# Two channel convolutions of a hybrid decoder block, done later in the gate turns

## The chip, the core and the metric

One core of one Trainium2 chip runs the whole block as one program. The metric is device time in microseconds (us), the median of several executions. Engine names are those of the profile: PE (TensorE matmuls), PEld (TensorE weight loads, which overlap PE), DVE (VectorE), ACT (ScalarE), POOL (GpSimd), SP (the engine that issues the weight loads).

## The reference, cut to what matters

For 256 tokens and 2048 channels, one block computes a Mamba-2 mixer and an S5 mixer in parallel, merges them by sigmoid gates, and runs a gated MLP. The change touches only the path of the Mamba-2 mixer's B and C inputs:

```python
z, xbc, dt_raw, u, g_a, g_b = jnp.split(hn @ w_in[i], splits, axis=-1)
xbc = jax.nn.silu(causal_dwconv(xbc, conv_w, conv_b))      # 4 taps per channel
xs, bm, cm = jnp.split(xbc, [D_INNER_A, D_INNER_A + gn], axis=-1)
cb = jnp.einsum("bclgn,bcsgn->bgcls", Cc, Bc)               # per group of 8
y_diag = jnp.einsum("bgcls,bgrcls,bcsgrp->bclgrp", cb, decay_in, X)
```

`bm` and `cm` have 8 groups of 128 channels each. Group g's product `cb` is needed for the first time when group g's part of the mixer runs.

## The kernel before, in words

**Weights.** All weights stream through a ring of four slots in units of 128 x 1024 fp32. SP loads a unit into `raw` once DVE has finished with the slot's last unit. ACT rounds it to `whi` (`split_hi`, line 666), DVE makes `wlo = raw - whi` (`split_lo`, line 1107), and PE multiplies with both (lines 1822 to 1824 in the gate phase, 1783 and 1785 before it). ACT and DVE work up to four units ahead of PE. Each engine runs its instructions strictly in the order in which the program lists them, and all waits are on semaphores.

**Order of the phases.** The projection `u`, then 24 groups `zx`, then 8 groups `bc` (each a B tile and a C tile, turns of four groups), then `gate` (8 turns of 8 units), `proj`, `glu`, `out`, `up`, `down`. During `zx` and `bc` the S5 scans run between the units on DVE. During `gate`, turn i also does the Mamba-2 mixer of group i.

**A `bc` group.** After PE has its sums, ACT copies one half out of PSUM (`hsum`, line 673) and DVE adds the halves (line 1112) into `cpad`, a tile with three zero columns ahead of the tokens. ACT computes the last tap with the bias (`group_tap`, line 776), from `cpad` into `bc`. DVE adds the other three taps for both tiles (`group_conv`, line 1303, six instructions). ACT applies Silu in place (`group_silu`, line 797). These pieces are listed one group behind: what belongs to group r stands in the turn of group r+1. Group 6's pieces stand in the last `bc` turn, group 7's in gate turn 0.

**A gate turn i.** In what follows "unit i.j" is unit j of gate turn i on PE. `hi(j)` and `lo(j)` in the code of turn i prepare the unit four later: `hi(0)` to `hi(3)` prepare i.4 to i.7, and `hi(4)` to `hi(7)` prepare (i+1).0 to (i+1).3. POOL loads the decay rows of three heads into each of two tiles (`dec`, line 442) as soon as PE has finished with them in the turn before. DVE scans them (`scan`, line 1416), ACT takes their exponential (line 853), DVE multiplies them with the masked `cb` (`blocks`, line 1422), PE forms the outputs (`heads`, lines 1908 and 1909), DVE adds the skip and multiplies by z (lines 1478 and 1481), ACT squares (line 895), DVE sums the squares (lines 1124 and 1486), and PE reduces them in the next turn behind its units 0 and 1 (`group_squares`, line 1829). ACT stages group i+1's B tile and x for PE (`stage`, lines 856 and 857), and PE makes `cb` and the transposes of x (lines 1924 to 1933) behind them. In gate turn 0, PE also finishes the last S5 block (`s5_products(7)`, line 1873) between its units 2 and 3; DVE's `s5_out` (line 1313) and ACT's first `stage` wait for it, and so does POOL with its second `dec` load.

The edit touches `group_tap`, `group_silu`, `stage` and `gate_turn` on ACT, `group_sums`, `group_conv`, `cpad_free` and `gate_turn` on DVE, and the operand of `cb` on PE.

Of the kernel before, what the change touches and what calls it, by code (L numbers as in the profile page):

```python
# [26 lines left out]
ds = bass.ds  # L27
# [81 lines left out]
def build_program(nc, a, out):  # L109
    ctx = ExitStack()  # L110
    with ctx:
# [77 lines left out]
        cpad = at("cpad", [P, 2, L + 4], F32, C + 4096)  # L189
        parm = at("parm", [P, N_PARM], F32, C + 6208)  # L190
# [465 lines left out]
        def _(act):  # L656
# [107 lines left out]
            def group_tap(name, i, r):  # L764

                _, per, quads, u0, g0 = phase(name)
                if name == "u" or name == "zx" and r % 2 == 0:
                    return
                act.wait_ge(sum_ready, i * per + (g0 + r + 1))
# [10 lines left out]
            def group_silu(name, i, r):  # L780
# [8 lines left out]
                elif name == "zx":  # L789
                    act.wait_ge(conv_done, i * 2 + (r // 2 + 1))  # L790
                    act.nop(nofuse=True)
                    to = zx[:, ds(i * 4 + (r - 1), 2), 1, :]
                    fn(to, to, ACTF.Silu).then_inc(xbc_done, 1)
                else:
                    act.wait_ge(conv_done, i * per + (12 + r + 1))
                    to = bc[:, ds(i * 4 + r, 1), :, :].rearrange("p o c n -> p (o c) n")
                    fn(to, to, ACTF.Silu).then_inc(xbc_done, 1)

# [45 lines left out]
            def gate_turn(i, prev, last=False):  # L844
# [10 lines left out]
                def stage(g):  # L855
                    fn(bst[:, :], bc[:, ds(g, 1), 0, :].rearrange("p o n -> p (o n)"), ACTF.Copy).then_inc(staged, 1)
                    fn(xst[:, :, :], zx[:, ds(g * TPG, TPG), 1, :], ACTF.Copy).then_inc(staged, 1)

                if prev is None:
# [10 lines left out]
                    group_silu("bc", 1, 3)  # L870
                    act.wait_ge(xbc_done, 20)
                    act.wait_ge(z_done, 12)
# [13 lines left out]
                hi(4)  # L886
                hi(5)
# [4 lines left out]
                hi(6)  # L892
                act.wait_ge(yz_ready, i + 1)
# [205 lines left out]
        def _(dve):  # L1099
# [215 lines left out]
            def group_sums(name, i, r):  # L1315
# [3 lines left out]
                elif name == "zx" and r % 2 == 0:  # L1319
                    add_halves(zx[:, ds(i * 4 + r, 2), 0, :], g0 + r, i * per)  # L1320
                else:
                    add_halves(cpad[:, :, 3:3 + L], g0 + r, i * per)

            def group_conv(name, i, r):
# [4 lines left out]
                if name == "u" or name == "zx" and r % 2 == 0:  # L1329
                    return  # L1330
                if name == "zx":
                    dve.wait_ge(tap_ready, i * 2 + (r // 2 + 1))
                else:
                    dve.wait_ge(tap_ready, i * per + (12 + r + 1))
# [6 lines left out]

            def cpad_free(name, i, r):

                if name == "bc":
                    dve.wait_ge(conv_done, i * 4 + (12 + r + 1))
# [60 lines left out]
            def gate_turn(i, prev, first_scan=False, next_scan=True):  # L1406
# [33 lines left out]
                if prev is None:  # L1440
# [4 lines left out]
                    group_conv("bc", 1, 3)  # L1445
# [23 lines left out]
                lo(4)  # L1469
                lo(5)  # L1470
                if prev is None:
                    dve.wait_ge(xbc_done, 20)
                    dve.wait_ge(z_done, 12)

# [278 lines left out]
        def _(pe):  # L1753
# [146 lines left out]
            def gate_turn(i, prev):  # L1900
# [22 lines left out]
                c = bc[:, ds(i, 1), 1, :].rearrange("p o n -> p (o n)")  # L1923
# [186 lines left out]
```

## Time and profile before

| | |
|---|---|
| median of 3 runs | 1679.96 us (1679.75 to 1681.75) |
| the profiled execution | 1680.3 us, of it 1678.6 us span |
| granted TensorE clock | 0.998 |
| PE busy | 1667.1 us, 99% |
| DVE busy | 1320.3 us, 79% |
| ACT busy | 962.7 us, 57% |
| gate turns 0 to 7 | from 431.7 to 641.7 us |

The profile is of one execution. A row of a timeline has the start, the time until the last of its instructions ended, the engine, the line, the operation and the tiles, and in square brackets how long the engine sat idle before it and what released it. Two instructions in a row on one engine can overlap a little, so the next start is often 0.1 us ahead of the last end.

### The profile page before, as it was taken

The page shows a single profiled execution, that of the slowest core. Times are in us where ns is not written, and L with a number is a line of the kernel's source. Part 1 is how long each engine was busy: PE and PEld are TensorE (multiplying, and loading weights), DVE is VectorE, ACT ScalarE, POOL GpSimd, SP SyncE. Part 2 cuts the span into 40 slices and gives each one's busy share as a digit, 9 for nine tenths or more (in the row PEclk, how much of TensorE's full clock was granted, in tenths as well). Part 3 has the DMA queues.
Part 4 walks back from the last instruction along what each step waited for, and adds up shares of the span by engine and source line. Part 5 has one row for each costly group of instructions (what it writes and reads, how often), then busy time and mean ns, then how long its engine had stood idle before and what let it go on. Part 6 is the DMA issues. An engine that isn't in the chain of part 4 may idle for free.

```text
span 1678.6 us, 24422 instructions
## 1 busy us (share of the span) xinstructions
PE 1667.1 (99%) x8340; PEld 1395.1 (83%) x8340; DVE 1320.3 (79%) x1685; ACT 962.7 (57%) x1271; POOL 216.4 (13%) x310
## 2 busy tenths in 40 slices
PE   9999999999999999999999999999999999999997
PEld 8888888888788888888888888888888888888886
DVE  7999999999998986545775868888878888845555
ACT  7676676766666667444557755444444444454553
POOL 7843342221000000000000200000000000000001
PEclk9999999999999999999999999999999999999999
DMA  7666766666666566656786577777777777666653
GB/s 254 213 197 199 204 206 200 193 188 190 194 217 231 191 219 189 199 191 201 239 254 232 174 233 241 243 241 244 242 244 241 245 232 248 225 194 195 191 189 123
DMA packets 174569, 358.49 MB, mean 214 GB/s; under 512 B 16880, under 2 KB 39584, under 8 KB 174368
## 3 DMA queue, kind: packets, MB, share of 16 engines
q1 hardware_dynamic: 162528, 338.26, 62.5%
q0 software_dynamic: 11248, 18.37, 4.6%
q8 instruction: 41, 0.67, 0.2%
q10 hardware_dynamic: 720, 0.93, 0.2%
q14 instruction: 32, 0.26, 0.0%
HBM read 335.41 MB, written 15.80 MB: 209 GB/s over the span
## 4 chain that ended last, share of the span: by engine, by line
PE 73%; DVE 2%; issue 0%; ACT 0%; DVEq 0%
PE psum L1822 22%; PE psum L1823 22%; PE psum L1824 22%; PE psum L1783 3%; PE psum L1785 2%; PE psum L1908 1%; DVE wlo L1107 0%; PE psum L1909 0%; DVE vn L1749 0%; PE psum L1933 0%; DVE bc L1303 0%; PE psum L1829 0%; PE psum L1924 0%; DVE dec L1416 0%; PE psum L1982 0%; PE psum L1979 0%
## 5 line engine op out<-in xcount | busy, mean ns | idle before, releaser
L1107 DVE TENSOR_TENSOR wlo<-raw,whi 128x1024 fp32r<-128x1024 f32 x580 | 709.6, 1230 | 321.3 <-ACT whi L666 314.0
L666 ACT ACTIVATE whi<-raw 128x1024 fp32r<-128x1024 f32 x580 | 611.9, 1058 | 577.1 <-PE psum L1824 455.1
L1783 PE MATMUL psum<-act,whi 128*128 128x512 f32 x1088 | 342.5, 396 | 0.0
L1822 PE MATMUL psum<-whi,nw 128*128 128x512 f32 x704 | 274.1, 389 | 0.0
L1824 PE MATMUL psum<-whi,nw 128*128 128x512 f32 x704 | 273.9, 389 | 0.0
L1823 PE MATMUL psum<-wlo,nw 128*128 128x512 f32 x704 | 273.9, 389 | 0.0
L1785 PEld LDWEIGHTS psum<-act,wlo 128*128 128x128 f32 x1088 | 204.4, 188 | 48.3
L1785 PE MATMUL psum<-act,wlo 128*128 128x256 f32 x1088 | 213.7, 278 | 0.0
L1783 PEld LDWEIGHTS psum<-act,whi 128*128 128x128 f32 x1088 | 165.6, 189 | 3.3 <-issue 2.8
L1824 PEld LDWEIGHTS psum<-whi,nw 128*128 128x128 f32 x704 | 132.1, 188 | 27.6
L1822 PEld LDWEIGHTS psum<-whi,nw 128*128 128x128 f32 x704 | 132.1, 188 | 27.3
L1823 PEld LDWEIGHTS psum<-wlo,nw 128*128 128x128 f32 x704 | 132.1, 188 | 27.3
L1822 PE MATMUL psum<-whi,act 128*128 128x512 f32 x352 | 138.8, 394 | 0.8 <-DVE wlo L1107 0.8
L1824 PE MATMUL psum<-whi,act 128*128 128x512 f32 x352 | 137.1, 390 | 0.0
L1823 PE MATMUL psum<-wlo,act 128*128 128x512 f32 x352 | 137.1, 389 | 0.0
L1822 PE MATMUL psum<-whi,ff 128*128 128x512 f32 x264 | 102.7, 389 | 0.0
L1823 PE MATMUL psum<-wlo,ff 128*128 128x512 f32 x264 | 102.7, 389 | 0.0
L1824 PE MATMUL psum<-whi,ff 128*128 128x512 f32 x264 | 102.7, 389 | 0.0
L1822 PEld LDWEIGHTS psum<-whi,act 128*128 128x128 f32 x352 | 66.1, 188 | 16.2 <-DVE wlo L1107 1.6
L1824 PEld LDWEIGHTS psum<-whi,act 128*128 128x128 f32 x352 | 66.1, 188 | 13.9
L1823 PEld LDWEIGHTS psum<-wlo,act 128*128 128x128 f32 x352 | 66.1, 188 | 13.1
L1303 DVE SCALAR_TENSOR_TENSOR fsum<-cpad,parm,fsum 128x256 f32<-128x256 f32 x176 | 76.9, 478 | 0.0
(251 smaller groups left out, 2300.3 us busy)
## 6 DMA issues: line engine op xcount, KB each, us to landing
raw<-in_w_up SPq DMA_DIRECT2D x176, 512.0 KB, 4.9
raw<-in_w_zx SPq DMA_DIRECT2D x96, 512.0 KB, 3.7
raw<-in_w_down SPq DMA_DIRECT2D x88, 512.0 KB, 3.8
raw<-in_w_gate SPq DMA_DIRECT2D x64, 512.0 KB, 5.6
raw<-in_w_proj SPq DMA_DIRECT2D x48, 512.0 KB, 4.4
raw<-in_w_bc SPq DMA_DIRECT2D x32, 512.0 KB, 3.7
raw<-in_w_glu SPq DMA_DIRECT2D x32, 512.0 KB, 4.4
raw<-in_w_out SPq DMA_DIRECT2D x32, 512.0 KB, 4.8
```

The lines of the kernel that those rows point to most:

```text
L666: fn(whi[:, s, :], raw[:, s, :], ACTF.Copy).then_inc(hi_ready, 1)
L1107: V.tensor_tensor(wlo[:, s, :], raw[:, s, :], whi[:, s, :], ALU.subtract).then_inc(lo_ready, 1)
L1303: ins = V.scalar_tensor_tensor(to[t], src, col(w, q * taps + k), to[t], ALU.mult, ALU.add)
L1783: mm(psum[:, b + t, :], whi[:, s, cols(t)], x, start=first, stop=False)
L1785: ins = mm(psum[:, b + t, L:2 * L], wlo[:, s, cols(t)], x[:, 0:L], start=False, stop=last)
L1822: mm(banks[:, t, :], x_hi, high[:, k], start=j == 0 and k == 0, stop=False)
L1823: mm(banks[:, t, :], x_hi, low[:, k], start=False, stop=False)
L1824: ins = mm(banks[:, t, :], x_lo, high[:, k], start=False, stop=last and k == 1)
L1908: mm(y, xtok[:, 0, x], dec[half][:, k, 0:L], start=True, stop=False)
```

## The change

Group 6 is no longer convolved in the last `bc` turn. Its sums go straight into the `bc` tile; in gate turn 1 ACT writes the last tap from there into `cpad` (`late_tap`, behind `hi(4)`), DVE adds the other taps out of place into `cpad` (`late_conv`, behind `lo(5)`), and ACT applies Silu to `cpad` (`late_silu`, behind `hi(6)`). Where group 6's B and C are used, in turns 5 and 6, they are read from `cpad`. Group 7's convolution moves on DVE from ahead of `lo(1)` to between `lo(4)` and `lo(5)` of gate turn 0, and its Silu on ACT from ahead of the first decay exponential to between `hi(4)` and `hi(5)`. The counts of the semaphores follow.

```diff
+        late_bc = {6: cpad}
+        late_count = {7: 7, 6: 8}
+        def bc_of(g, t):
+            return late_bc[g][:, t, 0:L] if g in late_bc else bc[:, g, t, :]
+        def bc_count(g):
+            return 12 + late_count.get(g, g + 1)
+        def comes_late(name, i, r):
+            return name == "bc" and i == 1 and r == 2
...
+            def late_tap(g):
+                act.wait_ge(sum_ready, phase("bc")[4] + g + 1)
+                for t in range(2):
+                    ins = fn(bc_of(g, t), bc[:, g, t, :], ACTF.Identity,
+                             scale=col("conv_a_w", (24 + 2 * g + t) * 4 + 3), bias=col("conv_a_b", 24 + 2 * g + t))
+                ins.then_inc(tap_ready, 1)
+            def late_silu(g):
+                act.wait_ge(conv_done, bc_count(g))
+                to = late_bc[g][:, :, 0:L]
+                fn(to, to, ACTF.Silu).then_inc(xbc_done, 1)
...
                     hi(1)
                     hi(2)
-                    group_silu("bc", 1, 3)
-                    act.wait_ge(xbc_done, 20)
-                    act.wait_ge(z_done, 12)
                     decay(0)
...
                 hi(4)
+                if i == 1:
+                    late_tap(6)
+                if prev is None:
+                    group_silu("bc", 1, 3)
+                    act.wait_ge(xbc_done, 19)
+                    act.wait_ge(z_done, 12)
                 hi(5)
...
                 hi(6)
+                if i == 1:
+                    late_silu(6)
                 act.wait_ge(yz_ready, i + 1)
...
+            def late_conv(g):
+                dve.wait_ge(tap_ready, bc_count(g))
+                for k in (2, 1, 0):
+                    for t in range(2):
+                        if k < 2:
+                            step.hold(but=1)
+                        to = bc_of(g, t)[:, 3 - k:L]
+                        ins = V.scalar_tensor_tensor(to, bc[:, g, t, 0:L - 3 + k],
+                                                     col("conv_a_w", (24 + 2 * g + t) * 4 + k), to, ALU.mult, ALU.add)
+                        if k or not t:
+                            step.begun(ins)
+                ins.then_inc(conv_done, 1)
...
                     scan(0)
-                    group_conv("bc", 1, 3)
                     lo(1)
...
                 lo(4)
+                if prev is None:
+                    group_conv("bc", 1, 3)
                 lo(5)
                 if prev is None:
-                    dve.wait_ge(xbc_done, 20)
+                    dve.wait_ge(xbc_done, 19)
                     dve.wait_ge(z_done, 12)
+                if i == 1:
+                    late_conv(6)
...
-                c = bc[:, ds(i, 1), 1, :].rearrange("p o n -> p (o n)")
+                c = bc_of(i, 1)
```

How instructions move is shown at three places. In these rows `wlo<-raw,whi` is a `split_lo`, `whi<-raw` a `split_hi`, `dec<-dec,mask` a scan of decay rows, `sx` and `st` are the S5 scan's tiles, and a row with x2 stands for two instructions.

DVE, end of the last `bc` turn and start of gate turn 0, before:

```order
L1107 TENSOR_TENSOR wlo<-raw,whi 128x1024 x2
L1303 SCALAR_TENSOR_TENSOR bc<-cpad,parm,bc 128x256 x6
L1278 SCALAR_TENSOR_TENSOR sx<-s5k,sx 128x256 x2
L1283 TENSOR_TENSOR st_78<-sx,tab_71 128x1024
L1289 TENSOR_TENSOR st_78<-st_78 128x512
L1107 TENSOR_TENSOR wlo<-raw,whi 128x1024 x2
L1112 TENSOR_TENSOR cpad<-psum,hsum 128x2x256
L1313 SCALAR_TENSOR_TENSOR ub<-ub,parm,psum 128x256
L1416 SCALAR_TENSOR_TENSOR dec_93<-dec_93,mask 128x384 x3
L1303 SCALAR_TENSOR_TENSOR bc<-cpad,parm,bc 128x256 x6
L1107 TENSOR_TENSOR wlo<-raw,whi 128x1024 x2
```

and now:

```order
L1138 TENSOR_TENSOR wlo<-raw,whi 128x1024 x2
L1309 SCALAR_TENSOR_TENSOR sx<-s5k,sx 128x256 x2
L1314 TENSOR_TENSOR st_78<-sx,tab_71 128x1024
L1320 TENSOR_TENSOR st_78<-st_78 128x512
L1138 TENSOR_TENSOR wlo<-raw,whi 128x1024 x2
L1143 TENSOR_TENSOR cpad<-psum,hsum 128x2x256
L1344 SCALAR_TENSOR_TENSOR ub<-ub,parm,psum 128x256
L1465 SCALAR_TENSOR_TENSOR dec_93<-dec_93,mask 128x384 x3
L1138 TENSOR_TENSOR wlo<-raw,whi 128x1024 x2
```

Both convolutions (the rows with `bc<-cpad,parm,bc`) are gone from this stretch.

ACT, from the middle of gate turn 0 to its end, before:

```order
L797 ACTIVATE bc<-bc 128x512
L853 ACT_TABLE_LOAD
L853 ACTIVATE dec_93<-dec_93 128x1152
L666 ACTIVATE whi<-raw 128x1024
L853 ACTIVATE dec_94<-dec_94 128x1152
L666 ACTIVATE whi<-raw 128x1024 x2
L856 ACTIVATE bst<-bc 128x256
L857 ACTIVATE xst<-zx 128x768
L666 ACTIVATE whi<-raw 128x1024
L895 ACTIVATE zx<-zx 128x3x256
```

and now:

```order
L879 ACT_TABLE_LOAD
L879 ACTIVATE dec_93<-dec_93 128x1152
L677 ACTIVATE whi<-raw 128x1024
L879 ACTIVATE dec_94<-dec_94 128x1152
L677 ACTIVATE whi<-raw 128x1024
L810 ACT_TABLE_LOAD
L810 ACTIVATE bc<-bc 128x512
L677 ACTIVATE whi<-raw 128x1024
L882 ACTIVATE bst<-bc 128x256
L883 ACTIVATE xst<-zx 128x768
L677 ACTIVATE whi<-raw 128x1024
L926 ACTIVATE zx<-zx 128x3x256
```

The Silu `bc<-bc` has gone from ahead of the exponentials to between the `split_hi` of units 1.0 and 1.1, with a table load of its own. In the same way ACT now has a table load ahead of the first exponential of turns 1 and 2, and one ahead of `late_silu`: four more than before.

DVE, second half of gate turn 1, before (the row with x2 is the `split_lo` of units 2.0 and 2.1, the last but one row that of unit 2.2):

```order
L1403 TENSOR_TENSOR y_hl<-zx,y_hl 128x3x256
L1107 TENSOR_TENSOR wlo<-raw,whi 128x1024 x2
L1478 SCALAR_TENSOR_TENSOR zx<-zx,parm,psum 128x256 x3
L1481 TENSOR_TENSOR zx<-zx 128x3x256
L1107 TENSOR_TENSOR wlo<-raw,whi 128x1024
L1124 TENSOR_TENSOR zx<-zx 128x256
```

and now:

```order
L1452 TENSOR_TENSOR y_hl<-zx,y_hl 128x3x256
L1138 TENSOR_TENSOR wlo<-raw,whi 128x1024 x2
L1385 SCALAR_TENSOR_TENSOR cpad<-bc,parm,cpad 128x255 x2
L1385 SCALAR_TENSOR_TENSOR cpad<-bc,parm,cpad 128x254 x2
L1385 SCALAR_TENSOR_TENSOR cpad<-bc,parm,cpad 128x253 x2
L1530 SCALAR_TENSOR_TENSOR zx<-zx,parm,psum 128x256 x3
L1533 TENSOR_TENSOR zx<-zx 128x3x256
L1138 TENSOR_TENSOR wlo<-raw,whi 128x1024
L1155 TENSOR_TENSOR zx<-zx 128x256
```

The three rows with `cpad<-bc,parm,cpad` are new. They stand ahead of the skip, the product with z and the squares' sum, and wait for `late_tap`, which on ACT stands between the `split_hi` of units 2.0 and 2.1.

## Rows read from the trace of the kernel before

**Rows 1.** The page, part 1: busy time of each engine.

```profile
PE 1667.1 (99%) x8340; PEld 1395.1 (83%) x8340; DVE 1320.3 (79%) x1685; ACT 962.7 (57%) x1271; POOL 216.4 (13%) x310
```

**Rows 2.** Busy time by stretch, 425 to 457.5 us (PE, PEld, DVE, ACT, POOL, clock, DMA).

```profile
425.00:457.50 32.50, 31.74 (x164) 25.49 (x163) 32.26 (x45) 21.85 (x31) 2.85 (x4) 1.00 0.65 206
```

**Rows 3.** Timeline of PEld, then of PE, gate turns 0 and 1.

```profile
440.07 0.62 PEld L1873 LDWEIGHTS psum<-st,cz 128*32 128x32 f32 x16 [0.36 <-issue]
441.14 0.19 PEld L1822 LDWEIGHTS psum<-whi,act 128*128 128x128 f32 x1 [0.45 <-DVE wlo L1107]
...
449.32 0.19 PEld L1822 LDWEIGHTS psum<-whi,act 128*128 128x128 f32 x1 [1.18 <-DVE wlo L1107]
...
465.56 0.60 PE L1829 MATMUL psum<-zx,ones 128*128 128x256 f32 x2
```

**Rows 4.** Timeline of DVE, last `bc` turn and gate turn 0.

```profile
434.25 2.46 DVE L1303 SCALAR_TENSOR_TENSOR bc<-cpad,parm,bc 128x256 f32<-128x256 f32 x6
...
439.26 0.69 DVE L1289 TENSOR_TENSOR st<-st 128x512 f32<-128x512 f32 x1
...
442.74 0.47 DVE L1313 SCALAR_TENSOR_TENSOR ub<-ub,parm,psum 128x256 f32<-128x256 f32 x1
...
448.05 2.35 DVE L1107 TENSOR_TENSOR wlo<-raw,whi 128x1024 fp32r<-128x1024 f32 x2
...
458.36 2.35 DVE L1107 TENSOR_TENSOR wlo<-raw,whi 128x1024 fp32r<-128x1024 f32 x2
...
464.38 0.43 DVE L1486 TENSOR_TENSOR zx<-zx 128x256 f32<-128x256 f32 x1
```

**Rows 5.** Timeline of ACT, gate turn 0 and, last, turn 1.

```profile
441.27 0.42 ACT L856 ACTIVATE bst<-bc 128x256 f32<-128x256 f32 x1 [1.51 <-issue]
...
442.92 1.09 ACT L776 ACTIVATE bc<-cpad,parm 128x256 f32<-128x256 f32 x2 [0.49 <-DVE cpad L1112]
443.92 1.99 ACT L666 ACTIVATE whi<-raw 128x1024 fp32r<-128x1024 f32 x2
...
448.82 1.28 ACT L853 ACT_TABLE_LOAD   x1
...
481.74 1.99 ACT L666 ACTIVATE whi<-raw 128x1024 fp32r<-128x1024 f32 x2
```

**Rows 6.** Timeline of DVE, gate turns 1 to 3.

```profile
482.87 2.35 DVE L1107 TENSOR_TENSOR wlo<-raw,whi 128x1024 fp32r<-128x1024 f32 x2
...
488.90 0.43 DVE L1486 TENSOR_TENSOR zx<-zx 128x256 f32<-128x256 f32 x1
...
500.88 1.22 DVE L1107 TENSOR_TENSOR wlo<-raw,whi 128x1024 fp32r<-128x1024 f32 x1
502.53 1.22 DVE L1107 TENSOR_TENSOR wlo<-raw,whi 128x1024 fp32r<-128x1024 f32 x1 [0.44 <-ACT whi L666]
...
527.94 1.22 DVE L1107 TENSOR_TENSOR wlo<-raw,whi 128x1024 fp32r<-128x1024 f32 x1
```

**Rows 7.** Timeline of PE (the last: PEld), gate turns 2 and 3.

```profile
491.46 0.60 PE L1829 MATMUL psum<-zx,ones 128*128 128x256 f32 x2
...
503.63 0.50 PE L1822 MATMUL psum<-whi,act 128*128 128x512 f32 x1
...
529.53 0.19 PEld L1822 LDWEIGHTS psum<-whi,act 128*128 128x128 f32 x1 [0.17 <-issue]
```

**Rows 8.** Timeline of POOL's decay loads, then of ACT behind weight loads.

```profile
504.36 0.53 POOL L442 DMA_DIRECT2D dec<-decay_rows  x1 [0.17 <-issue]
...
608.45 0.53 POOL L442 DMA_DIRECT2D dec<-decay_rows  x1 [0.61 <-PE psum L1909]
...
513.49 1.06 ACT L666 ACTIVATE whi<-raw 128x1024 fp32r<-128x1024 f32 x1 [4.64 <-DMA raw<-in_w_gate]
...
616.95 1.06 ACT L666 ACTIVATE whi<-raw 128x1024 fp32r<-128x1024 f32 x1 [1.51 <-DMA raw<-in_w_gate]
```

**Rows 9.** DMA issues between 432 and 446 us: KB each, median us to landing.

```profile
dec<-decay_rows POOLq DMA_DIRECT2D x2, 576.0 KB, 5.6
```

More of the change, by code:

```diff
@@ L768, in group_tap @@
                     return
+                if comes_late(name, i, r):
+                    return
                 act.wait_ge(sum_ready, i * per + (g0 + r + 1))
@@ L793, in group_silu @@
                     fn(to, to, ACTF.Silu).then_inc(xbc_done, 1)
-                else:
-                    act.wait_ge(conv_done, i * per + (12 + r + 1))
+                elif not comes_late(name, i, r):
+                    act.wait_ge(conv_done, bc_count(i * 4 + r))
                     to = bc[:, ds(i * 4 + r, 1), :, :].rearrange("p o c n -> p (o c) n")
                     fn(to, to, ACTF.Silu).then_inc(xbc_done, 1)
+            def late_tap(g):
[8 more added lines that the diff above has]
+                fn(to, to, ACTF.Silu).then_inc(xbc_done, 1)
             def mixer_turn(name, i, blk, prev):
@@ L855, in stage @@
                 def stage(g):
-                    fn(bst[:, :], bc[:, ds(g, 1), 0, :].rearrange("p o n -> p (o n)"), ACTF.Copy).then_inc(staged, 1)
+                    fn(bst[:, :], bc_of(g, 0), ACTF.Copy).then_inc(staged, 1)
                     fn(xst[:, :, :], zx[:, ds(g * TPG, TPG), 1, :], ACTF.Copy).then_inc(staged, 1)
@@ L1320, in group_sums @@
                     add_halves(zx[:, ds(i * 4 + r, 2), 0, :], g0 + r, i * per)
+                elif comes_late(name, i, r):
+                    add_halves(bc[:, i * 4 + r, :, :], g0 + r, i * per)
                 else:
@@ L1330, in group_conv @@
                     return
+                if comes_late(name, i, r):
+                    return
                 if name == "zx":
@@ L1333, in group_conv @@
                 else:
-                    dve.wait_ge(tap_ready, i * per + (12 + r + 1))
+                    dve.wait_ge(tap_ready, bc_count(i * 4 + r))
                 if name == "zx":
@@ L1340, in group_conv @@
                     conv_pair(to, i * 8 + (24 + 2 * r), 4, "conv_a_w", "conv_a_b", conv_done, True)
+            def late_conv(g):
[10 more added lines that the diff above has]
+                ins.then_inc(conv_done, 1)
             def cpad_free(name, i, r):
-                if name == "bc":
-                    dve.wait_ge(conv_done, i * 4 + (12 + r + 1))
+                if name == "bc" and not comes_late(name, i, r):
+                    dve.wait_ge(conv_done, bc_count(i * 4 + r))
                 elif name == "zx" and r % 2:
```

## The prediction

> **What bounds the kernel now.** Read the page's busy times first: PE is busy for 1667.1 us of the span, and no other engine above 79% [rows 1]. Only what makes PE stop can be won back, or lost. The waits and PEld's timeline around the edit show where PE stops: for 0.45 us at 441.14 before unit 0.3, whose `wlo` came late, and for 1.18 us at 449.32 before unit 0.5, for the same reason; at 440.07 PE also began the last S5 products 0.36 us late, right after DVE's row at 439.26 had ended [rows 3, 4]. The table of stretches says why: from 425 to 457.5 us DVE is busy for 32.26 of 32.50 us [rows 2]. Here DVE is the engine that everything queues behind, for a short while. The change takes two convolutions out of this stretch and puts them in later, so the question is what the later places have room for.
>
> All that follows is a replay of the three queues in the new order: each instruction starts when the one before it on its engine has let go and the one that it waits for has ended. Durations are those of the rows; from one start to the next a convolution takes 2.38 us (434.25 to the scan behind it), a `split_lo` 1.13 us (half of the pair at 448.05), and a `split_hi` 0.95 us [rows 4, 5]. "Lag" is how much later something happens than before; minus is earlier.
>
> **Gate turn 0, first half: the gain.** With group 6's convolution gone from 434.25, all of DVE's rows behind it come 2.4 us earlier. The S5 products start right behind unit 0.2 (-0.36), unit 0.3 no longer waits (-0.45), and unit 0.5 doesn't either (-1.18). PE is then 2.0 us ahead (0.36 + 0.45 + 1.18) at the end of unit 0.7. DVE can't keep its own lead in full. `s5_out` would start at 440.4 (442.74 - 2.4), but the products end about 1.2 us after they start (440.07 to ACT's row at 441.27), at 440.9: a new wait of 0.6 us. ACT's `stage` waits for the same, then does the tap (1.09 us) and the `split_hi` of 0.5, which so ends at 444.1; DVE, ahead by the second convolution too, waits 0.2 us for it [rows 3 to 5]. The second scan needs the second decay load. It is issued when the products end and lands some 5.6 us later [rows 9], which is 0 to 0.7 us after DVE wants it, at about 446.3. I take 0.4, since it will share the queues with fewer weight loads than before, and keep both ends.
>
> **Gate turn 0, second half: the gain is given back.** Group 7's convolution now stands between `lo(4)` and `lo(5)`, which were the pair at 458.36. Its Silu on ACT can only start then, and the `split_hi` of unit 1.1 is queued behind that Silu, and DVE's `lo(5)`, the very next instruction behind the convolution, needs it. So DVE does nothing for one Silu and one `split_hi`: 1.7 us, at about 0.6 us (one pass over a 128x512 tile at half the price of the 128x1024 of a `split_hi`) and 1.04 us. This is the new wait that the diff creates. The table load ahead of the Silu (1.28 us) runs while ACT waits for the convolution: behind the second scan ACT has an exponential and a `split_hi`, some 2.1 us, and DVE has all that lay between 453.0, where that scan ended (2.6 us behind the pair at 448.05), and 458.36, then `lo(4)` and the convolution, 8.9 us. If ACT came late there, the load would cost its full length. DVE's sum for the turn: -2.4 (group 6's gone) + 0.6 + 0.2 + 0.4 + 1.7 (waits) is +0.5 (group 7's convolution is in the turn before and after). The squares' sum that ended at 464.8 then ends at 465.3 [rows 4, 5]. PE, 2.0 us ahead of its 465.3, is at `group_squares(0)` at 463.3, and stands still until then. Before, it began these matmuls at about 465.3 too (465.56 in PE's row, the weight load 0.25 us earlier) [rows 3]. **The 2.0 us are gone; PE's lag is 0.1.**
>
> **Gate turn 1: a loss.** Nothing is added ahead of `hi(4)` but a table load, which falls into a wait of ACT for the scan. From `hi(4)` on: ACT's `late_tap` of 1.0 us lets DVE wait some 0.75 us for the `split_hi` of unit 2.1 (the second of DVE's pair at 482.87 started 0.27 us behind the end of ACT's pair at 483.73, and 1.0 us is now put in between). Then comes group 6's convolution, 2.4 us, ahead of the skip, the product with z and the squares. DVE's lag at the end of the second squares' sum is 0.5 + 0.75 + 2.4 = 3.6 us: 489.33 (488.90 + 0.43) becomes 492.95. PE arrives there at 491.2 (the weight load ahead of 491.46) and before had 1.9 us to spare [rows 6, 7]. **It now stands still: lag 3.6 - 1.9 + 0.1 for the signal = 1.8 us.** `late_silu` and its table load fit: ACT waits for the convolution, and the product with z takes longer than the Silu.
>
> **Gate turn 2.** DVE has no idle time to catch up with. Its `split_lo` for unit 2.5 ended at 502.10 and PE started there at 503.63, so PE had 1.5 us to spare; with DVE 3.5 us late (of its 3.6 it wins 0.1 from a short wait) PE's lag becomes 2.0 us [rows 6, 7]. The exponential's extra table load lies ahead of an ACT row whose result DVE wants 3 us later.
>
> **Gate turn 3.** PE has only 0.37 us to spare at unit 3.5 (529.16 against 529.53) [rows 6, 7]. But here the chain starts anew: ACT waits 4.64 us for the weights of unit 3.2 to land, at 513.49, and DVE behind it. They were issued when DVE ended the `split_lo` of 2.6, at 503.75, that is 0.6 us before the second decay load was issued at 504.36, and landed 9.1 us after that decay load. In turn 7 the second decay load was issued at 608.45 and the weights landed at 616.95, 8.5 us after it, although they were issued behind it [rows 6, 8]. So, as I read the two rows, what sets the landing is the decay load, which PE starts, not the weights' own issue. The decay load lags by PE's 2.0 us; the weights then land at most 2.0 us later than before, rather than DVE's 3.5, and nothing is added. From there on DVE, which idles in turns 3 to 7, follows PE.
>
> **The sum** is +0.1 (turn 0), +1.7 (turn 1), +0.2 (turn 2), 0 after: 2.0 us slower. No DMA is added or removed; PE's matmul on `cpad` is the same matmul; late taps read 255, 254 and 253 columns in place of 256, at the same price. The profiled execution took 1680.3 us, 1.7 us around its span of 1678.6 us, so one like it would take 1682.3; against the median of 1679.96 I predict 1682.0.
>
> **Rivals.**
> 1. *The gain stays.* The waits on DVE in turn 0 are shorter than I make them, and turn 1 hides the convolution behind its 1.9 us to spare and shorter waits. For it: the slack is real. Against it: three items of known length (0.75, 2.4 and what turn 0 leaves) exceed it. Time: 1680.0 - 2.0 = 1678.0.
> 2. *The loads of turn 3 follow the weights' own issue, not the decay load.* Then DVE's lag of 3.5 us holds through turn 3, the 0.37 us at unit 3.5 are eaten, and PE's lag grows from 2.0 to about 3.4 us, once: 1683.4, on the other side of the bound. It decides when the weights of 3.2 are held up by more than 2.4 us (2.0 + 0.37). For it: only two landings are compared above. The Trainium skill (DMA: Bandwidth & Descriptors, Queues, rings and completion order) says that each DMA engine takes turns between the queues that have work, a packet at a time; by that rule the weights get a share from their own issue on and a later issue means a later landing. The landing 9.1 us behind a decay load issued later than they were does not contradict the rule, and one comparison of two turns does not refute it.
> 3. *A wash.* The wait for the second decay load is 0, DVE is even at turn 0's end, and turn 1's tap hides behind ACT's wait for `y_hl`: PE loses 0.5 us or less. Against: the tap stands behind that wait. Time: 1680.4.
>
> **Chances.** Forecast 0.47, rival 1 0.15, rival 2 0.23, rival 3 0.15. A change of 0.2%, 3.4 us, is about what a measurement of this kernel can tell from none. Only rival 2 reaches it, and only half of its outcomes, with the upper end (0.7 us) of the decay load's wait on top in some; a gain of 3.4 us isn't there to be had, since only 2.0 us of stalls are removed. So faster 0.02, same 0.85, slower 0.13. The range goes from rival 1's 1678.0 to 1683.8 (rival 2 with the upper end of that wait).
>
> **What would show it.** Right: PEld has no idle time at units 0.3 and 0.5; ACT waits over 5 us for the convolution in turn 0 and DVE 1.7 us for `whi` behind it; PE waits for DVE's L1538 (the squares' sum) about 1.5 us in turn 0's chain and 1.7 us in turn 1's; from turn 3 on all rows stand 2.0 us later than before. Wrong: no wait at the second sum of squares (rival 1 or 3), or a new one at unit 3.5 (rival 2).

## The result and the profile after

The changed kernel takes 1682.98 us (median of 20 runs, 1682.08 to 1684.1), the kernel before 1680.13 us on the same chip (median of 20, 1679.73 to 1682.97). By the medians it is slower by 2.85 us. The ratio, over all runs compared, is 1.0015 with a 95% interval of 1.0009 to 1.0021, which is 1.5 to 3.5 us: slower, by 0.09 to 0.21%. The profiled execution took 1682.71 us, its span is 1681.1 us, 2.5 us more than before.

First the totals (the page of the changed kernel, part 1), to be held against [rows 1]:

```profile
PE 1666.8 (99%) x8340; PEld 1393.9 (83%) x8340; DVE 1320.8 (79%) x1685; ACT 967.6 (58%) x1275; POOL 216.4 (13%) x310
```

PE has the same work, DVE 0.5 us more, and ACT 4.9 us more, which is the four new table loads (4 x 1.28 us = 5.1). So the 2.5 us are time in which PE stands still. Where it does shows in PEld's timeline around the edit:

```profile
440.15 0.59 PEld L1925 LDWEIGHTS psum<-st,cz 128*32 128x32 f32 x16 [0.35 <-issue]
441.16 0.19 PEld L1874 LDWEIGHTS psum<-whi,act 128*128 128x128 f32 x1 [0.41 <-issue]
...
448.24 0.19 PEld L1874 LDWEIGHTS psum<-whi,act 128*128 128x128 f32 x1
...
465.53 0.30 PEld L1881 LDWEIGHTS psum<-zx,ones 128*128 128x128 f32 x2 [1.35 <-DVE zx L1538]
...
493.16 0.30 PEld L1881 LDWEIGHTS psum<-zx,ones 128*128 128x128 f32 x2 [1.87 <-DVE zx L1538]
...
503.44 0.20 PEld L1960 LDWEIGHTS psum<-dec,xtok 128*64 128x64 f32 x4 [0.49 <-ACT rs L688]
...
504.58 0.35 PEld L1960 LDWEIGHTS psum<-dec,xtok 128*64 128x64 f32 x4
...
506.03 0.19 PEld L1874 LDWEIGHTS psum<-whi,act 128*128 128x128 f32 x1 [0.17 <-issue]
```

Against [rows 3] and [rows 7]: unit 0.5 starts at 448.24 without the wait of 1.18 us, 1.08 us earlier than before. The two rows at 440.15 and 441.16 stand where they stood. At 465.53 and 493.16 PE waits for L1538, the sum of the squares. The first time that makes it as late as before (the matmul was at 465.56), the second time 1.7 us later (it was at 491.46). Unit 2.5 starts at 506.03 (503.63 before).

DVE's timeline shows what it was doing instead:

```profile
436.93 0.69 DVE L1320 TENSOR_TENSOR st<-st 128x512 f32<-128x512 f32 x1
...
441.30 0.48 DVE L1344 SCALAR_TENSOR_TENSOR ub<-ub,parm,psum 128x256 f32<-128x256 f32 x1 [0.80 <-PE psum L1925]
...
455.91 2.46 DVE L1334 SCALAR_TENSOR_TENSOR bc<-cpad,parm,bc 128x256 f32<-128x256 f32 x6
460.15 1.23 DVE L1138 TENSOR_TENSOR wlo<-raw,whi 128x1024 fp32r<-128x1024 f32 x1 [1.79 <-ACT whi L677]
...
465.05 0.43 DVE L1538 TENSOR_TENSOR zx<-zx 128x256 f32<-128x256 f32 x1
...
485.42 1.23 DVE L1138 TENSOR_TENSOR wlo<-raw,whi 128x1024 fp32r<-128x1024 f32 x1 [0.66 <-ACT whi L677]
486.56 2.45 DVE L1385 SCALAR_TENSOR_TENSOR cpad<-bc,parm,cpad 128x255 f32<-128x255 f32 x6
...
492.68 0.42 DVE L1538 TENSOR_TENSOR zx<-zx 128x256 f32<-128x256 f32 x1
...
501.90 2.63 DVE L1471 TENSOR_TENSOR dec<-dec,cbm 128x1152 f32<-128x1152 f32 x2
504.45 1.22 DVE L1138 TENSOR_TENSOR wlo<-raw,whi 128x1024 fp32r<-128x1024 f32 x1
```

The row at 436.93 was at 439.26 [rows 4], 2.3 us earlier. By 465.05 nothing of this is left: the last row of the squares' sum was at 464.38 [rows 4], so DVE is 0.67 us late, after a new wait of 0.80 us at `s5_out` and one of 1.79 us behind the convolution. The rest are some 0.2 us ahead of the `split_lo` of unit 0.5 (at 444.46), and the 0.1 us or so by which DVE's rows overlap where it does not wait. In turn 1 DVE waits 0.66 us for the `split_hi` behind the tap, then convolves: the second squares' sum is at 492.68 (488.90 before, [rows 6]), 3.8 us late.

ACT's timeline has the middle link of the wait of 1.79 us, and the end of DVE's lag in turn 3:

```profile
451.56 1.28 ACT L810 ACT_TABLE_LOAD   x1
458.40 0.63 ACT L810 ACTIVATE bc<-bc 128x512 f32<-128x512 f32 x1 [5.56 <-DVE bc L1334]
459.06 1.06 ACT L677 ACTIVATE whi<-raw 128x1024 fp32r<-128x1024 f32 x1
...
515.15 1.06 ACT L677 ACTIVATE whi<-raw 128x1024 fp32r<-128x1024 f32 x1 [2.47 <-DMA raw<-in_w_gate]
```

ACT stands at the Silu for 5.56 us, though unit 1.1's weights could have been rounded in that time, and DVE, once it has convolved, waits for both (458.40 to 460.12). The chain of waits of the changed kernel (start, duration, what) goes right through both convolutions:

```profile
455.99 2.39 DVE bc L1334 x6
458.40 0.64 ACT bc L810
459.06 1.07 ACT whi L677
...
486.64 2.37 DVE cpad L1385 x6
```

PE's lag, as the difference of the first weight loads of a unit between two traces, is followed in this way through all the kernels below (us; minus is earlier than before; the ratio compares the runs with those of the kernel before, with its 95% interval):

| kernel | unit 0.5 | 1.2 | 2.2 | 2.5 | 3.5 | 7.7 | span, difference | ratio |
|---|---|---|---|---|---|---|---|---|
| the changed kernel | -1.08 | +0.08 | +1.80 | +2.40 | +2.42 | +1.94 | +2.5 | 1.0015 (1.0009 to 1.0021) |
| g7_only | -1.12 | +1.30 | +1.33 | +1.33 | +1.68 | +1.19 | +1.2 | 1.0007 (0.9998 to 1.0016) |
| g6_only | -1.15 | -1.18 | -0.37 | +0.23 | +0.25 | +0.69 | +1.5 | 0.9999 (0.999 to 1.0008) |
| silu_behind | -1.13 | -1.16 | +0.16 | +0.76 | +0.77 | +0.29 | +0.3 | 1.0001 (0.9992 to 1.001) |
| g6_turn2 | -1.25 | +0.03 | +0.05 | +0.05 | +0.15 | +0.32 | +0.5 | 1.0001 (0.9992 to 1.001) |
| root_first | -0.97 | +0.56 | +2.28 | +2.88 | +2.89 | +3.16 | +3.5 | 1.0016 (1.0007 to 1.0025) |
| both_moves | -1.08 | -1.11 | -1.11 | -1.11 | -0.94 | -0.91 | -0.7 | 0.9992 (0.9983 to 1.0001) |
| both_late | -1.27 | -1.30 | -1.30 | -1.30 | -1.30 | -1.43 | -0.9 | 0.9995 (0.9986 to 1.0004) |
| moves_and_root | -0.95 | -0.98 | -0.98 | -0.98 | -0.41 | -0.90 | -0.9 | 0.9996 (0.9987 to 1.0005) |
| late_issue | -1.26 | -1.29 | -1.29 | -1.29 | +0.27 | -0.21 | -0.2 | 0.9997 (0.9987 to 1.0006) |

The columns bracket the places: 1.2 lies right behind the first matmul of squares, 2.2 behind the second, 2.5 behind turn 2's heads. All ten kernels take a convolution away ahead of unit 0.5 and get -0.95 to -1.27 there: so far apart are lags that mean the same. The difference was there before: at unit 0.4 the lags are between -0.13 and +0.18, and from unit 0.4 to unit 0.5 every one of the ten kernels gains 1.13 or 1.14 us. Behind turn 5 small waits of a single execution add up to more, so for the sign of half a microsecond I go by the ratios and not by the spans.

### The profile page after: what moved, and what is told of

Same layout as the page of the kernel before. It is cut to its first block, busy times and chain, and to the rows that moved or that the text cites. A ratio compares the mean times of both kernels' runs of the same rounds, so it can differ in the third digit from the quotient of the medians.

```text
span 1681.1 us, 24424 instructions
## 1 busy us (share of the span) xinstructions
PE 1666.8 (99%) x8340; PEld 1393.9 (83%) x8340; DVE 1320.8 (79%) x1685; ACT 967.6 (58%) x1275; POOL 216.4 (13%) x310
## 4 chain that ended last, share of the span: by engine, by line
PE 71%; DVE 4%; ACT 1%; issue 1%; DMA 1%; SPq 0%; DVEq 0%; ACTq 0%
PE psum L1874 21%; PE psum L1875 21%; PE psum L1876 21%; PE psum L1835 5%; PE psum L1837 2%; DVE wlo L1138 1%; DVE dec L1465 1%; PE psum L1960 1%; ACT whi L677 0%; DMA quad_m<-merged_blocks 0%; DVE bc L1334 0%; DVE vn L1801 0%; PE psum L1961 0%; DMA merged_blocks<-flat_m 0%; PE psum L1881 0%
```

## Experiments

Each edit is shown against the changed kernel. The first four shared the runs of the kernel before (median 1680.6 of 33), the next four another set (1680.54 of 33), the last its own (1680.34 of 13).

### g7_only: only group 7's convolution moves

```diff
-        late_bc = {6: cpad}
-        late_count = {7: 7, 6: 8}
+        late_bc = {}
+        late_count = {}
...
         def comes_late(name, i, r):
-            return name == "bc" and i == 1 and r == 2
+            return False
...
-                if i == 1:
-                    late_tap(6)
...
-                if i == 1:
-                    late_conv(6)
```

> Only group 7's convolution and Silu move (behind the fifth low part of turn 0); group 6 is convolved in the last bc turn as before. Theory (new wait on the Silu in turn 0, late squares in turn 1 come from group 6 alone): the stall before unit 0.5 is gone (about -1.1 us), DVE then waits 1.7 us for the high part of unit 1.1 and, since nothing is taken out for group 6, ends the first squares' sum 1.7 us later than before; PE waits about 2.3 us for it and lags by 1.2 us; no wait at the second squares' sum. In all +1.2 us (0.07%) in the gate phase. Rival (the loss of the whole change is group 6's convolution in turn 1): this one is 1.1 us faster than before.

Measured: 1681.79 us, against 1680.6. With group 6 convolved as before, DVE is 2.4 us later in turn 0, and the same wait behind group 7's convolution follows (timeline of DVE, then of PEld):

```profile
461.38 1.22 DVE L1134 TENSOR_TENSOR wlo<-raw,whi 128x1024 fp32r<-128x1024 f32 x1 [1.79 <-ACT whi L677]
```

```profile
466.75 0.30 PEld L1875 LDWEIGHTS psum<-zx,ones 128*128 128x128 f32 x2 [1.50 <-DVE zx L1532]
```

PE falls from -1.12 to +1.30 at the first sum of squares and gets nothing added there in turn 1. Group 7's part alone costs about 1.2 us by the medians and by the trace (the interval of its ratio just reaches 1): what it saves at unit 0.5 is less than what the Silu chain costs. The 0.35 us at unit 3.5 are a wait of another kind, which root_first below explains.

### g6_only: only group 6's convolution moves

```diff
                     hi(2)
+                    group_silu("bc", 1, 3)
+                    act.wait_ge(xbc_done, 19)
+                    act.wait_ge(z_done, 12)
                     decay(0)
...
                     scan(0)
+                    group_conv("bc", 1, 3)
                     lo(1)
...
-                if prev is None:
-                    group_conv("bc", 1, 3)
                 lo(5)
```

> Only group 6 moves (turn 1, out of place); group 7 stays where it was before. Theory: DVE runs 1.4 us ahead through turn 0, so both the stall before unit 0.5 and the wait at the first squares' sum are absent (PE -1.1 us); in turn 1 the wait for the tap and the convolution put the second squares' sum 1.7 us later than before, PE waits 0.9 us for it, and ends turn 1 at about -0.1 us; turn 2 adds 0.1. In all 0 us within 0.4. Rival (group 6's convolution in turn 1 is what costs, at its full 2.4 us whatever turn 0 does): +1.3 us or more.

Measured: 1680.44 us against 1680.6. The gain at unit 0.5 (-1.15) passes the first sum of squares, and half of it is lost at the second, where PE waits for DVE (PEld's timeline):

```profile
490.99 0.30 PEld L1879 LDWEIGHTS psum<-zx,ones 128*128 128x128 f32 x2 [0.97 <-DVE zx L1536]
```

The rest goes at unit 2.5, 0.6 us where 0.1 were expected. What is lost behind turn 4 (+0.25 at unit 3.5, span +1.5) are small waits of this one execution; the median doesn't show them. Each half of the change takes about the same wait at unit 0.5 away: doing both wins it once and pays for both.

### silu_behind: the changed kernel with group 7's Silu one place later

```diff
                 hi(4)
...
+                hi(5)
                 if prev is None:
                     group_silu("bc", 1, 3)
                     act.wait_ge(xbc_done, 19)
                     act.wait_ge(z_done, 12)
-                hi(5)
```

> The whole change, but group 7's Silu on ACT stands behind the high part of unit 1.1 instead of ahead of it. Theory: DVE's wait of 1.8 us ahead of the low part of unit 1.1 vanishes, PE doesn't wait at the first squares' sum and keeps its -1.1 us; at the second one it waits 1.2 us (DVE +2.0 us there) and is at +0.1; turn 2 adds 0.1 to 0.3. In all +0.3 us against before, 2.1 us less than the changed kernel in the gate phase. Rival (DVE is simply full and the order on ACT doesn't matter): +2 us or more, as the changed kernel.

Measured: 1680.97 us, where the changed kernel has 2.85 us above its kernel before and this one 0.4. DVE's row that waited 1.79 us (timeline of DVE) has no wait, and PE waits in turn 1 alone (timeline of PEld):

```profile
458.53 1.22 DVE L1138 TENSOR_TENSOR wlo<-raw,whi 128x1024 fp32r<-128x1024 f32 x1
```

```profile
491.52 0.30 PEld L1881 LDWEIGHTS psum<-zx,ones 128*128 128x128 f32 x2 [1.49 <-DVE zx L1538]
```

The two intervals against the kernel before touch (1.0009 to 1.0021 for the change, 0.9992 to 1.001 here), so it is the rows that decide: the wait in turn 0 is not the price of the convolution's place on DVE, but of one line's place on ACT. What is left, +1.3 us from unit 1.2 to 2.2 and +0.6 at 2.5, is the price of group 6's place in turn 1.

### g6_turn2: the changed kernel with group 6's convolution in turn 2

```diff
-                if i == 1:
-                    late_tap(6)
...
                     stage(i + 1)
+                if i == 2:
+                    late_tap(6)
                 hi(6)
-                if i == 1:
-                    late_silu(6)
...
                 fn(gates[:, i, :, :], chunk_banks("gate", i), ACTF.Copy).then_inc(gate_free, 1)
+                if i == 2:
+                    late_silu(6)
...
-                if i == 1:
-                    late_conv(6)
...
                 V.tensor_tensor(zx[:, q, 1, :], zx[:, q, 1, :], zx[:, q, 0, :], ALU.mult).then_inc(yz_ready, 1)
+                if i == 2:
+                    late_conv(6)
```

> The whole change, but group 6's tap, convolution and Silu stand in gate turn 2, where DVE waited 3.2 us for a weight load before: the convolution behind the product with z, the tap ahead of the last but one high part, the Silu behind the copy of the gate sums. Theory: turn 0 is as in the changed kernel (PE +0.1 us behind the first squares' sum), turn 1 has no wait at the second one, turn 2 hides the 2.4 us in DVE's wait. In all +0.1 us against before, within 0.4. Rival (table loads and DVE's total work carry the loss, wherever the convolution stands): +2 us as in the changed kernel.

Measured: 1680.82 us against 1680.6. The wait at the first sum of squares is as in the changed kernel, the second is gone (both rows from PEld's timeline):

```profile
465.48 0.30 PEld L1881 LDWEIGHTS psum<-zx,ones 128*128 128x128 f32 x2 [1.47 <-DVE zx L1538]
...
491.28 0.42 PEld L1881 LDWEIGHTS psum<-zx,ones 128*128 128x128 f32 x2
```

Either loss appears without the other. Their sizes do not quite add up: from unit 1.2 to 2.2 silu_behind loses 1.32 us, the changed kernel 1.72, since there DVE comes late out of turn 0 as well.

### root_first: what holds unit 2.5?

In turn 2 of the changed kernel PE's lag grew by 0.6 us, not by the 0.2 us of the prediction, and the heads' row at 503.44 names ACT's logarithm (`rs`, L688). The edit puts that logarithm and its table loads ahead of the second exponential.

```diff
-                    decay(1)
-                    group_root(prev)
+                    if i == 2:
+                        group_root(prev)
+                        decay(1)
+                    else:
+                        decay(1)
+                        group_root(prev)
```

> The whole change, but in gate turn 2 ACT does the root (logarithm and exponential, with their table loads) ahead of the second decay exponential instead of behind it. Theory (the 0.6 us that the changed kernel loses in turn 2 are PE's wait for that logarithm, which frees the bank of the sums): PE's lag at unit 2.5 falls from 2.4 to 2.1 us, where the low part of unit 2.5, 0.36 us ahead of PE so far, becomes the limit. Rival (as the prediction had it, DVE's low part or the products with the masked decay set that wait): it stays at 2.4 us or grows.

Measured: 1683.25 us against 1680.54, as the changed kernel. The logarithm was done early, the heads' first row waits for nobody, and yet the step at 2.5 is the same 0.60 us (+2.28 to +2.88). The theory of the logarithm fell. The heads of this kernel show what it is (timelines of DVE, then PEld):

```profile
502.38 2.63 DVE L1475 TENSOR_TENSOR dec<-dec,cbm 128x1152 f32<-128x1152 f32 x2
```

```profile
503.86 0.23 PEld L1964 LDWEIGHTS psum<-dec,xtok 128*64 128x64 f32 x4 [0.44 <-issue]
...
505.06 0.29 PEld L1964 LDWEIGHTS psum<-dec,xtok 128*64 128x64 f32 x4
...
506.51 0.18 PEld L1878 LDWEIGHTS psum<-whi,act 128*128 128x128 f32 x1 [0.17 <-issue]
```

DVE's second masked product (`blocks(1)`) ended at 505.01, the heads' second half started at 505.06, and unit 2.5 at 506.51, 1.50 us after the product. In the changed kernel it is 504.53, 504.58 and 506.03: again 0.05 and 1.50. The heads' 24 loads, undisturbed, have unit 3.5 start 2.15 us after their first (527.38 to 529.53 before); here it is 2.65, in the changed kernel 2.59. So what binds is the product, through the heads' second half, and not the `split_lo` behind it, which ended at 505.67 in the changed kernel, 0.36 us ahead of PE. In the code the heads' second half waits for this product.

The other traces say the same. From turn 2 on no unit 5 of a gate turn, in any of the eleven kernels, starts less than 1.49 us behind the end of that turn's second product. In turns 2 and 3, where PE's lag grows at that unit, it is 1.49 or 1.50: unit 2.5 of g6_only, silu_behind, root_first and the changed kernel, unit 3.5 of g7_only, g6_turn2, both_moves, moves_and_root and late_issue. Where it doesn't, it is up to 2.9 us.

This execution also had the only wait for the second decay load, 0.27 us (timeline of DVE):

```profile
447.21 2.66 DVE L1469 TENSOR_TENSOR_SCAN dec<-dec,mask 128x384 f32<-128x384 f32 x3 [0.27 <-DMA dec<-decay_rows]
```

It is why its lag at 1.2 is +0.56.

### both_moves: silu_behind and g6_turn2 together

The edit is the sum of the two diffs above.

> The two edits of silu_behind and g6_turn2 together: group 7's Silu behind the high part of unit 1.1, group 6 in gate turn 2. Theory: each removes one of the two waits at a sum of squares, and the stall before unit 0.5 stays away, so PE is 1.1 us ahead of the kernel before through turns 0 to 3 and keeps it: -1.1 us, within 0.5. Rival (the waits only move on to turn 2 or 3): 0 us or more.

Measured: 1679.46 us against 1680.54, ratio 0.9992 (0.9983 to 1.0001). Both waits at the squares are gone and PE keeps the -1.1 us; 0.17 us go at unit 3.5, which starts 1.50 us behind the masked product. The convolution lies in the time in which ACT and DVE wait for unit 3.2's weights anyway (timelines of ACT, then of DVE):

```profile
512.56 1.06 ACT L677 ACTIVATE whi<-raw 128x1024 fp32r<-128x1024 f32 x1 [3.68 <-DMA raw<-in_w_gate]
```

```profile
510.44 2.45 DVE L1385 SCALAR_TENSOR_TENSOR cpad<-bc,parm,cpad 128x255 f32<-128x255 f32 x6
513.66 1.23 DVE L1138 TENSOR_TENSOR wlo<-raw,whi 128x1024 fp32r<-128x1024 f32 x1 [0.77 <-ACT whi L677]
```

2.4 us of convolution, and DVE still has 0.77 us to wait behind it.

### both_late: group 7 goes to turn 3 as well

```diff
-        late_bc = {6: cpad}
-        late_count = {7: 7, 6: 8}
+        late_bc = {6: cpad, 7: hsum}
+        late_count = {}
...
-            return name == "bc" and i == 1 and r == 2
+            return name == "bc" and i == 1 and r >= 2
...
+                if i in (2, 3):
+                    late_tap(i + 4)
                 hi(6)
...
+                if i in (2, 3):
+                    late_silu(i + 4)
...
+                if i in (2, 3):
+                    late_conv(i + 4)
                 lo(6)
```

> Groups 6 and 7 both late and out of place: group 6 in gate turn 2 into cpad, group 7 in gate turn 3 into hsum, which nothing else uses during the gate turns. Theory: PE has no DVE stall left to give back in turn 0 beyond the 1.1 us, so this gives -1.1 us as both_moves does, although DVE has another 2.4 us less in turn 0. Rival (DVE's load in turn 0 is itself the price): clearly more than 1.1 us of gain.

Measured: 1679.35 us, as both_moves. Nothing of either convolution is left in turn 0, and DVE even idles there (timeline of DVE):

```profile
458.88 1.26 DVE L1524 SCALAR_TENSOR_TENSOR zx<-zx,parm,psum 128x256 f32<-128x256 f32 x3 [2.18 <-PE psum L1957]
```

PE gains no more by it: from unit 0.4 to unit 0.5 1.14 us, as in all the others. That is all there was to win in turn 0, not the 2.0 us of the prediction.

### moves_and_root: both_moves, and the logarithm first in all turns

Besides the edits of both_moves:

```diff
                     hi(1)
+                    group_root(prev)
                     decay(1)
-                    group_root(prev)
                     hi(2)
```

> both_moves with the root ahead of the second decay exponential in all gate turns from 1 on. Theory: in turns where weight loads land late (turn 6 of the kernel before) PE waits up to 0.5 us for the logarithm; this removes it: -1.1 to -1.6 us. Rival (the second exponential then comes 1.4 us late and DVE's products with it): -1.1 us or worse, with PE waiting for the products.

Measured: 1679.59 us; no gain over both_moves, a miss. PE is 0.57 us later at unit 3.5 (-0.98 to -0.41), and is back at -0.9 at the end of the gate turns. The rival names what takes the 0.57 us: DVE waits for the second exponential, now behind the logarithm (timeline of DVE, turn 3):

```profile
526.27 1.36 DVE L1471 TENSOR_TENSOR dec<-dec,cbm 128x1152 f32<-128x1152 f32 x1 [1.35 <-ACT dec L879]
```

That masked product ends at 527.63, and unit 3.5 starts 1.49 us later, at 529.12. What comes back in turn 6 is not the logarithm's either (see "not foreseen" below), so the theory had next to no wait to win.

### late_issue: are the weights held by their own issue or by the decay load?

Rival 2 again, by an intervention: in both_moves three idle DVE operations on `hsum` (which is free there) are put ahead of the `split_lo` whose end lets SP load unit 3.2.

```diff
+                    if i == 2:
+                        for _ in range(3):
+                            step.done(V.tensor_tensor(hsum[:, :, :], hsum[:, :, :], hsum[:, :, :], ALU.max))
                     lo(2)
```

> both_moves with three idle operations of DVE (maxima of hsum with itself, some 2.1 us in all) ahead of the low part of unit 2.6, so that the load of unit 3.2's weights is issued 2.1 us later while the decay loads of turn 3 stay where they are. Theory (the decay loads set when those weights land): they still land 9 us behind the second decay load, at about 512.5 us of the span, within 0.7, and unit 3.5 starts within 0.3 us of where it does in both_moves. Rival (the weights share the queues from their own issue on): they land about 2 us later, at 514.6, and PE's lag grows by about 1.5 us at unit 3.5.

Measured: the `split_lo` ended 2.07 us later than in both_moves (504.96 against 502.89), so the weights were issued that much later. The decay loads were issued as before. Timelines of late_issue: DVE, POOL and ACT.

```profile
501.56 2.13 DVE L1515 TENSOR_TENSOR hsum<-hsum 128x512 f32<-128x512 f32 x3
503.73 1.22 DVE L1138 TENSOR_TENSOR wlo<-raw,whi 128x1024 fp32r<-128x1024 f32 x1
```

```profile
503.07 0.53 POOL L453 DMA_DIRECT2D dec<-decay_rows  x1 [0.17 <-issue]
```

```profile
511.36 1.06 ACT L677 ACTIVATE whi<-raw 128x1024 fp32r<-128x1024 f32 x1 [0.41 <-DMA raw<-in_w_gate]
```

and POOL's row in both_moves:

```profile
503.25 0.53 POOL L453 DMA_DIRECT2D dec<-decay_rows  x1 [0.17 <-issue]
```

Issued 2.07 us later, the weights landed 1.2 us *earlier* (ACT took them at 511.36 and at 512.56), 8.3 us behind the second decay load (9.3 in both_moves). By rival 2's rule they would have landed at about 514.6, 11.5 us behind it, and no landing of turns 3 to 7 in the eleven kernels is more than 9.9 us behind. That side is refuted, though by one execution. That the decay load sets the landing is not shown by it: the loads behind that of unit 3.2 went out later too, and could have left it more room. The other half of the expectation missed: unit 3.5 was to stay within 0.3 us and came 1.21 us later than in both_moves (+0.27 against -0.94). All of DVE's rows were 2 us late, so the convolution started at 512.51, the `split_lo` of 3.2 at 514.88 (513.66 in both_moves), and the wait for the weights was no longer long enough to hide both. PE lost 0.96 us at the sum of the squares ahead of unit 3.2 (timeline of PEld) and 0.6 us at unit 3.5, which started 1.49 us behind the masked product:

```profile
516.94 0.30 PEld L1884 LDWEIGHTS psum<-zx,ones 128*128 128x128 f32 x2 [1.10 <-DVE zx L1541]
```

## Why the prediction came out right

The forecast was 1682.0, the result 1682.98 in a range of 1678.0 to 1683.8: 1 us above the forecast, and a change below 0.2% as forecast. It is not a change that the measurement can't tell from none, as the prediction had it for all below 0.2%: the ratio's interval is 0.12% wide and leaves out 1. The path was the one forecast (gain at unit 0.5, given back at the first squares' sum, loss at the second, turn 3 adds nothing). Of the signs that it named one failed: PEld still has idle time at unit 0.3. The terms one by one:

- **Gain in turn 0, 2.0 us: over-sized, 1.1 measured.** The 1.18 us at unit 0.5 were real (1.08 won). The 0.36 and 0.45 us around the S5 products were not stalls that DVE's lead could end. With `st` ready 2.3 us earlier, PEld's rows still have 0.35 and 0.41 us, both now put down to "issue". That the S5 products began "right after DVE's row at 439.26 had ended" was a coincidence. both_late, with DVE idle, shows the same limit. The kernel before showed it too, in PE's own timeline: of the three places PE stands still at one alone.

```profile
440.10 1.07 PE L1873 MATMUL psum<-st,cz 128*32 128x256 f32 x16
441.14 0.50 PE L1822 MATMUL psum<-whi,act 128*128 128x512 f32 x1
...
449.32 0.50 PE L1822 MATMUL psum<-whi,act 128*128 128x512 f32 x1 [0.76 <-DVE wlo L1107]
```

The prediction added up the idle time of the weight loads, which can pause while PE still works through its matmuls. PE's busy time in [rows 2], 31.74 of 32.50 us, has the same 0.76 us; in the changed kernel it is all of the 32.50.

- **DVE's waits in turn 0: right in kind.** `s5_out` 0.80 (0.6 forecast), the `split_hi` of unit 0.5 about 0.2 (0.2), Silu and `split_hi` 1.79 (1.7), 0 for the decay load (0.4 taken, 0 to 0.7 allowed; 0.27 in one run). DVE ends the turn 0.67 us late (0.5), PE 0.08 (0.1). That the over-sized gain did no harm is luck of the path: the first sum of squares gives it back whatever it is, where DVE comes out of turn 0 early, PE keeps its gain, and the 0.9 us too much would have shown in the time. silu_behind is such a kernel, and it shows the cause of the wait of 1.79 us: one Silu out of the chain, and it is gone.
- **Turn 1: right.** Wait behind the tap 0.66 (0.75), the convolution 2.4, DVE 3.8 us late (3.6), PE's lag +1.72 (+1.7).
- **Turn 2, +0.2: under-sized, +0.6 measured.** The step that failed is "its `split_lo` for unit 2.5 ended at 502.10 and PE started there at 503.63, so PE had 1.5 us to spare". PE does not meet the `split_lo` first, but the masked product ahead of it, whose end the heads need 1.50 us ahead of unit 2.5 (root_first). Before (timeline of DVE, turn 2 and then turn 3), the product ended at 499.61 + 1.35 = 500.96:

```profile
499.61 1.35 DVE L1422 TENSOR_TENSOR dec<-dec,cbm 128x1152 f32<-128x1152 f32 x1
...
525.39 2.63 DVE L1422 TENSOR_TENSOR dec<-dec,cbm 128x1152 f32<-128x1152 f32 x2
```

So the spare was 503.63 - 500.96 - 1.50 = 1.17 us; DVE's lag there is 504.53 - 500.96 = 3.57, and 3.57 - 1.17 = 2.40, PE's lag to the hundredth. root_first: 505.01 - 500.96 - 1.17 = 2.88, again as measured. In the same way the 0.37 us "to spare at unit 3.5" were none: the product ended at 528.02, 1.51 us ahead of PE's 529.53, where 1.50 are needed.
- **Turn 3, nothing added: right.** DVE's lag is cut by the wait for the weights, as forecast; that it is the decay load that times them fits the rows and is not shown. The decay load went out 2.40 us later (504.36 before), the weights 3.57 us later, and they landed 1.66 us later (513.49 before, [rows 8]). The row of POOL in the changed kernel:

```profile
506.76 0.53 POOL L453 DMA_DIRECT2D dec<-decay_rows  x1 [0.61 <-PE psum L1961]
```

- **Not foreseen, both small.** At unit 6.5 the lag falls by 0.46 us. The profile names ACT's logarithm for PEld's 0.38 us ahead of that turn's heads in the kernel before, but 0.35 us stand there with nobody late. It was the masked product again: it ended at 606.22, and unit 6.5 started 1.49 us later (timelines of DVE and PEld, before); in the changed kernel these are 1.91 us.

```profile
603.59 2.63 DVE L1422 TENSOR_TENSOR dec<-dec,cbm 128x1152 f32<-128x1152 f32 x2
607.71 0.19 PEld L1822 LDWEIGHTS psum<-whi,act 128*128 128x128 f32 x1 [0.17 <-issue]
```

And at the start of `out` PE waits some 0.6 us in this execution, for DVE; its cause was not tried. The two nearly cancel in the span. By the medians the change costs 2.85 us, and PE's lag at the end of the gate turns is 1.94: that the sum of 2.0 us comes so near to the latter is in part luck (turn 2 is 0.4 short, turn 6 gives 0.46 back), and some 0.9 us of the former were not traced beyond this wait. PEld's timeline of the changed kernel at that place:

```profile
881.35 0.19 PEld L1874 LDWEIGHTS psum<-whi,act 128*128 128x128 f32 x1 [0.62 <-DVE act L1595]
```

- **Rivals.** Rival 1 (the gain stays) and rival 3 (a wash) failed at both sums of squares. Rival 2 (the loads follow their own issue) fails on the changed kernel, with +2.42 at unit 3.2 and +2.42 at 3.5, and on late_issue. Its price was also summed wrongly: a lag of 3.5 us less 0.37 us to spare is 3.1, not 3.4 us. The Trainium skill (DMA: Bandwidth & Descriptors, Queues, rings and completion order) says that each DMA engine takes turns, packet by packet, between the queues for which it has work; the rival's reading of it, that a later issue means a later landing, is not what these landings show (511.36 against 512.56). No run here shows the turns themselves, or tells what holds the weights up.

Only one wait of some 1.2 us was to be won in turn 0, and both convolutions' new places lie on the path from DVE to a matmul of squares that PE has little time to spare for. both_moves, with both put where an engine waits for a DMA or for nothing, is 1.08 us below the kernel before, and both_late 1.19. Their intervals lie below that of the changed kernel, so that they beat it is shown; each reaches just over 1, so that they beat the one before is likely at best.

## What to carry to other kernels

An instruction that ACT takes from DVE, placed ahead of what DVE wants next from ACT, makes a loop: both engines then stand still for each other's work, one Silu and one `split_hi` here, and one line's place decides it. Moved work should go to where its engine waits for a transfer (turn 2's wait of over 3 us swallowed 2.4 us of convolution), not just later. To know what a stall is worth, read it in PE's own rows and not in those of the weight loads, and take off what the same kind of transition costs where nobody is late. Measure the slack of PE from everything that it needs, each with its own lead time, and not only from what DVE finished last.

## What was not expected of the hardware

- PEld stands still ahead of each group of narrower loads (the 128x32 of the S5 products, the 128x64 of the heads) with nobody late, and no edit here took it away: 0.33 us at six of the eight S5 products in each of the eleven kernels and 0.35 or 0.36 at the last, never less than 0.35 at the heads. Where it is more, something else comes on top (0.49 us at 503.44 in the changed kernel). PE's own rows at 440.10 and 441.14 have no idle time ahead of them.
- The load of a turn's unit 2, issued beside the two decay loads (576 KB each), lands 8.4, 8.1, 8.9, 8.7 and 8.7 us behind the issue of the second one in turns 3 to 7 of the changed kernel, and 8.3 us in late_issue, where the weights were issued 1.9 us behind it. In 54 of the 55 such landings of the eleven kernels it is 7.6 to 9.9 us. The exception is moves_and_root in turn 3, where the weights were issued 1.35 us ahead of it and landed 6.0 us behind it: a head start of that size seems to be kept, while one of 0.6 us (9.1 us in the kernel before) or 1.0 us (8.9 us in silu_behind, turn 6) is not. Why is open.
- The table load (1.28 us) is carried out while the `ACTIVATE` behind it has to wait anyway (451.56, then 5.56 us of waiting), and costs nothing there; where ACT isn't waiting the `ACTIVATE` behind it starts at once, as 494.88 + 1.28 to 496.17 in the changed kernel.
